# A two-layer transformer kernel: the second layer's first weight loads no longer wait for the gathered expert results

## The reference

```python
for i in range(DEPTH):                                   # DEPTH = 2
    sh1, sc1, ga1, sh2, sc2, ga2 = ada_chunks(c, w_ada[i], b_ada[i])
    h_l = modulate(rmsnorm(x, g_norm1[i]), sh1, sc1)     # latent tokens
    h_c = modulate(rmsnorm(ctx, g_norm1[i]), csh1, csc1) # context tokens
    out_l, out_c = token_mixer(h_l, h_c, w_in[i], ..., w_out[i], cos, sin, not last)
    x = x + ga1 * out_l
    h2_l = modulate(rmsnorm(x, g_norm2[i]), sh2, sc2)
    y = moe(...)        # y += gates[:, e] * ((silu(h@w_e_gate[e]) * (h@w_e_up[e])) @ w_e_down[e])
    x = x + ga2 * y     # layer 0 does the same for ctx
return rmsnorm(x, g_final)
```

## Time and profile before

| | |
|---|---|
| median of the runs | 1664.7 us (1659.17 to 1667.28) |
| the profiled execution's own time | 1660.41 us |
| its span in the trace | 1658.6 us |
| busy: PE, DVE, ACT, POOL | 90%, 63%, 53%, 8% of the span |
| chain that ended last, by engine | PE 79%, DVE 8%, DMA 6%, ACT 3%, issue 2% |
| mean granted TensorE clock | 0.942 of full speed |

### The profile page before, as it was taken

The page is one execution under the profiler, slowest core; times in us unless marked ns, Lnnn a source line. Parts: engine busy times, 40 slices in busy tenths (PEclk is TensorE's granted clock), DMA queues, the critical chain, the costliest instruction groups (busy, mean ns, idle before and its releaser), DMA issues.

```text
span 1658.6 us, 22446 instructions
## 1 busy us (share of the span) xinstructions
PE 1485.5 (90%) x7758; PEld 1124.5 (68%) x7758; DVE 1037.8 (63%) x1487; ACT 878.2 (53%) x1310; POOL 126.9 (8%) x106
## 2 busy tenths in 40 slices
PE   5889999998879987999999739999999779999993
PEld 2577777776557846788888618988758556666662
DVE  2312334322885437999999554653486479999994
ACT  4323122223774233888888526423475458887882
POOL 1100000000000000111111010000000011211201
PEclk8799999999999996999999978999999879999997
DMA  8752665566002314999999472642404269999992
GB/s 287 273 177 103 240 245 212 202 212 221 1 10 88 112 45 173 361 384 386 378 376 367 158 253 90 204 139 90 139 1 142 88 234 388 363 363 373 369 331 85
DMA packets 129997, 359.21 MB, mean 217 GB/s; under 512 B 15217, under 2 KB 15538, under 8 KB 129282
## 3 DMA queue, kind: packets, MB, share of 16 engines
q1 hardware_dynamic: 117522, 323.20, 54.0%
q0 software_dynamic: 11536, 31.87, 5.3%
q10 hardware_dynamic: 864, 3.15, 0.5%
HBM read 346.62 MB, written 26.21 MB: 225 GB/s over the span
## 4 chain that ended last, share of the span: by engine, by line
PE 79%; DVE 8%; DMA 6%; ACT 3%; issue 2%; SPq 1%; POOL 1%; POOLq 0%; ACTq 0%; DVEq 0%
PE ps L507 22%; PE ps L508 22%; PE ps L509 22%; PE ps L710 3%; DVE amax L1410 2%; PE ps L728 2%; PE ps L932 2%; DMA w_raw<-in_w_gate 2%; PE ps L796 1%; DMA w_raw<-in_w_in 1%; PE ps L816 1%; PE ps L886 1%; DVE att_a L1319 1%; PE ps L768 1%; PE ps L919 1%
## 5 line engine op out<-in xcount | busy, mean ns | idle before, releaser
L503 DVE TENSOR_TENSOR w_lo<-w_raw,w_hi 128x1024 fp32r<-128x1024 f32 x320 | 386.9, 1223 | 387.9 <-ACT w_hi L499 380.7
L499 ACT ACTIVATE w_hi<-w_raw 128x1024 fp32r<-128x1024 f32 x320 | 336.8, 1059 | 449.2 <-PE ps L509 198.1
L507 PE MATMUL ps<-h_hi,w_hi 128*128 128x512 f32 (+1 forms) x704 | 251.5, 357 | 18.9 <-DVE h_lo L1335 9.1
L509 PE MATMUL ps<-h_hi,w_lo 128*128 128x512 f32 (+1 forms) x704 | 248.0, 352 | 0.0
L508 PE MATMUL ps<-h_lo,w_hi 128*128 128x512 f32 (+1 forms) x704 | 247.9, 352 | 0.0
L503 DVE TENSOR_TENSOR w_lo_more<-w_raw,w_hi_more 128x1024 fp32r<-128x1024 f32 x192 | 231.4, 1223 | 13.6 <-ACT w_hi_more L499 4.8
L499 ACT ACTIVATE w_hi_more<-w_raw 128x1024 fp32r<-128x1024 f32 x192 | 202.1, 1059 | 42.4 <-PE ps L509 42.4
L507 PEld LDWEIGHTS ps<-h_hi,w_hi 128*128 128x128 f32 x704 | 134.8, 192 | 44.4 <-issue 10.8
L509 PEld LDWEIGHTS ps<-h_hi,w_lo 128*128 128x128 f32 x704 | 134.7, 191 | 18.6
L508 PEld LDWEIGHTS ps<-h_lo,w_hi 128*128 128x128 f32 x704 | 134.9, 192 | 18.2 <-issue 0.2
L507 PE MATMUL ps<-w_hi,xg_hi 128*128 128x512 f32 (+1 forms) x256 | 104.5, 408 | 8.4 <-DVE xg_lo L1611 8.4
(11 more groups left out here) (238 smaller groups left out, 2521.8 us busy)
## 6 DMA issues: line engine op xcount, KB each, us to landing
w_raw<-in_w_e_gate SPq DMA_DIRECT2D x128, 512.0 KB, 5.6
w_raw<-in_w_e_up SPq DMA_DIRECT2D x128, 512.0 KB, 7.0
w_raw<-in_w_e_down SPq DMA_DIRECT2D x128, 512.0 KB, 6.0
w_raw<-in_w_ada SPq DMA_DIRECT2D x96, 512.0 KB, 6.8
w_raw<-in_w_in SPq DMA_DIRECT2D x56, 512.0 KB, 3.7
w_raw<-in_w_gate SPq DMA_DIRECT2D x32, 512.0 KB, 7.1
w_raw<-in_w_attn_out SPq DMA_DIRECT2D x16, 512.0 KB, 3.5
w_raw<-in_w_out SPq DMA_DIRECT2D x16, 512.0 KB, 3.6
```

Of the source, the lines that this page charges most:

```text
L499: act.activation(whi(n), raw[:, slot(n), :, :], ACT.Copy).then_inc(hi_ready, 1)
L503: dve.tensor_tensor(wlo(n), raw[:, slot(n), :, :], whi(n).bitcast(F32), ALU.subtract).then_inc(lo_ready, 1)
L507: pe.matmul(acc, sh, mh, start=first, stop=False, skip_group_check=True)
L509: return pe.matmul(acc, sl, mh, start=False, stop=last, skip_group_check=True)
```

## The change

Two lines of SyncE's program go: the wait ahead of the second layer's loads. Every load keeps its own wait for room in the ring.

```diff
         for i in range(DEPTH):
-            if i:
-                sp.wait_ge(y_in[3], 32 * i)
             for n, (s, ch) in enumerate(stream_of(i)):
                 if i == 0 and n < WS:
                     continue
                 load(sp, mix0[i] + n, chunk_of(i, s, ch))
```

## The result

| | before | changed |
|---|---|---|
| median, first measurement | 1661.73 us (5 runs, 1659.17 to 1667.28) | 1653.34 us (5 runs, 1649.35 to 1653.68) |
| span of the profiled execution | 1658.6 us | 1647.5 us |
| ratio, 95% interval | | 0.9937 (0.9917 to 0.9957) |

The changed kernel is faster, by 0.6% in this measurement. Twice more on other occasions, with more runs of before beside it, the ratio was 0.9964 (0.9945 to 0.9982) and 0.9962 (0.9948 to 0.9976).

The account below looks back on a forecast made before the run. TensorE matmuls bound the kernel (79% of the chain of waits); between the layers ScalarE's late splits held the norm. 5.2 us earlier start plus 1.3 from the clock make 6.5: 1664.7 - 6.5 = 1658.2, named 1658, range 1651.5 to 1664.

Parts of the forecast that it names:

- Start and landing of the loads: Between the layers, eight of SyncE's weight loads move to 926 to 936, four stay; their DMA backlog is gone by about 941.
- ScalarE: Before the second layer's norm, its four weight splits run from about 948.7, 1.06 us each, and leave the chain of waits.
- The first sum right behind the transposes (5.2 us): Second layer's norm: TensorE's first sum starts at about 975.45, after the transposes, instead of 980.61; 5.2 us won.
- The pace of the sums (1.3 us): The norm's eight sums run faster because TensorE's clock is already up; 1.3 us of the 6.5 us gain at `std`.
- VectorE's `w_lo` hidden: VectorE's four `w_lo`, 977.80 to 982.4, end 1.5 us before `std` is done at 983.9, so they cost nothing.
- Store held up: Rival: early loads share engines with expert 15's store, making it 2.3 us late; gain only 4.2, 1660.5 us; chance 0.08.
- Collision: Rival: the eight loads fly during the gathers, 953 to 968, adding up to 11.2 us; 1669.4 us; chance 0.04.
- Nothing changed behind `std`: After the second layer's norm root, order and distances stay the same, so what is won there arrives at the end.
- What a measurement can tell from no change, and the chances: Whole time: about 0.5%, 8.3 us, is distinguishable from no change; faster 0.33, within 0.62, slower 0.05.
- The base of the time named: Whole time: 6.5 us off the runs' median 1664.7 gives 1658.2, named 1658; off the profiled 1660.41 it gives 1653.9.

Follow-up runs that it names:

- the filled gap: Kernel before, with five matmuls of constants added on TensorE between the last transpose and the first sum; 1658.77 us, ratio 0.9986 (0.9971 to 1.0002).

## Why the prediction was right and where it was wrong

- **Start and landing of the loads.** Right: 924.74 and the DMA engines free by 940, for 926 and 941 forecast; eight loads moved, four stayed. This whole trace runs 1.5 us earlier than that of before already where the change begins.
- **ScalarE.** Right: four splits at 947.23, forecast 948.7; they left the chain.
- **The first sum right behind the transposes (5.2 us).** Right in place. In size, over three traces of before and four changed, the distance from the first transpose to the first sum fell from 10.4 to 5.7, 4.7 us. The transposes took 5.1 to 6.7 us over these traces, with the clock at 0.71 over the 5.2 us of the first changed one and at 0.50 for the first 5.5 of the 6.6 of the second of before.
- **The pace of the sums (1.3 us).** Right in cause, shown by the filled gap; too small. It was read from the one trace in which the sums took 9.1 us. The first pair of traces gives 1.5; in the two other traces of before they took 10.5, and in the mean the pace was worth 2.4 us. Together 7.1 us, forecast 6.5, and gather to Fourier step gives the same: 60.3 less 53.2, 7.0 us.
- **VectorE's `w_lo` hidden.** Right, 1.17 us to spare, forecast 1.5.
- **Store held up.** Did not happen: the stores at 938.86 and 946.50 keep the distance of the earlier trace rows, and the next gather followed as before. The two stores and the first gather landed in 2.6 to 4.2 us.
- **Collision.** Did not happen, but made on purpose it cost 5.4 to 5.8 us.
- **Nothing changed behind `std`.** Right up to the Fourier step: 22.1 to 22.9 us before, 22.0 to 22.9 changed. Behind it the first pair differed by 2.6 us, the means by 1.0; open.
- **What a measurement can tell from no change, and the chances.** This step was wrong. I took 0.5%, 8.3 us, for it, found the gain of 6.5 us inside, and so gave 0.62 to "within" and 0.33 to faster. The runs told far smaller differences: the interval of the first measurement reaches 3.3 us to either side of its ratio, those of the two longer ones 3.1 and 2.3, and none of the three holds no change (upper ends 0.9957, 0.9982, 0.9976). Against such an interval a gain of 6.5 us is clear of no change, and faster was the outcome to name. In size the two longer measurements give 0.36% and 0.38%, 6.0 and 6.3 us, as the mechanism has it. What the first has above that, 0.63%, did not return; it was scatter, or in part the open piece behind the Fourier step.
- **The base of the time named.** I had 1653.9 from the profiled execution, 6.5 less than its 1660.41, and then took 1658 from the median of three runs. The kernel before has a median of 1659.9 to 1660.9 in sets of 12, 20 and 30 runs, so the three runs stood about 4 us too high, and the trace's own base was the better one: 1653.34 was measured. That it came within 0.6 us of 1653.9 is partly luck, since that measurement's gain was above the mechanism's. The base does not bear on faster or not: 6.5 us are 0.39% of either.
- **The 11.1 us between the first two profiles.** 1.5 us of it lay in front of the change (the first gather issued at 951.5 instead of 953.0, at the same distance from the last expert load), 7.0 in the stretch, 2.6 behind it. Only the middle one returns in every pair of traces, at 5.7 to 8.1 us.

## What to carry to other kernels

A load's start matters to whatever stands behind its consumer in that engine's program: here four splits of weights that nobody needed yet held the squares of a norm, and TensorE behind them, and once it stood still its clock made the next matmuls slower too. Before moving a load earlier, look for a hole in the DMA share that is large enough for it: the same eight loads held up neither the stores nor the gathers when they ran from 925 to 940, and cost 5 to 6 us beside the gathers. Before calling a gain too small to be measured, compare it with the interval that such runs give, here 2 to 3 us to either side. Take the size of a small gain from distances between fixed instructions in several traces of both kernels; the end of the unchanged first layer moved by as much as the gain, 7 us.

## What the runs showed of the hardware that was not expected

TensorE's products of 128x256 in the second layer run at one of two paces at a granted clock of 1.00, constant over one execution's stretch. The stretch of 139 us that starts 21 us behind the Fourier step's first matmul, in the first trace of before, the first changed, the second of before and the fourth changed:

```profile
1033.60:1172.60 139.00, 139.00 (x795) 121.69 (x794) 69.05 (x123) 48.58 (x62) 0.58 (x1) 1.00 0.43 137
```

```profile
1025.10:1164.10 139.00, 139.00 (x802) 122.01 (x801) 69.36 (x123) 48.83 (x63) 0.58 (x1) 1.00 0.43 137
```

```profile
1037.30:1176.30 139.00, 139.00 (x802) 122.00 (x801) 69.35 (x123) 48.85 (x63) 0.58 (x1) 1.00 0.43 137
```

```profile
1027.10:1166.10 139.00, 139.00 (x796) 121.69 (x796) 69.10 (x122) 48.59 (x62) 0.58 (x1) 1.00 0.44 137
```

795 or 796 matmuls against 802 in the same time, starts of neighbouring products 120.0 ns apart or 118.6, and each kernel shows both. Of all 14 traces nine have the slower pace and five the faster, with traces of before and of the changed kernel on either side. In the first two traces it looked like a further microsecond won by the change; the later ones show that it is not tied to it. Its cause is open.
